# A hybrid attention, recurrence and expert layer: gate map written to PSUM token by token, and the token rows loaded behind the ring in the last stage

## Chip, core and metric

The kernel runs on one core of one Trainium2 chip. The metric is the time of one execution on the device in microseconds, as the median of several runs.

## What is computed

The layer mixes 1024 tokens of width 1024 (attention over a neighbourhood, a recurrence, gates), and then sends each token through PEER: product keys choose 16 of 16384 single-neuron experts for each of 8 heads. The part that matters here is the second:

```python
expert = jnp.take_along_axis(cand_i, pos, axis=-1)          # (token, head, 16)
gate = jax.nn.softmax(best_s, axis=-1)
...
act = jax.nn.gelu(jnp.einsum('td,thkd->thk', hc, u[ec]))    # u: 16384 x 1024
return jnp.einsum('thk,thkd->td', gc * act, v[ec])          # v: 16384 x 1024
...
x = x + gate2[:, None, :] * y
```

## The kernel before

Everything is float32. A product of high precision is made of three matmuls on operands that are split into a high and a low part (`product3`, lines 80 to 82): ScalarE copies the high part, VectorE subtracts it for the low one.

The experts form a 128 x 128 grid, so expert number = 128 x chunk + place. Of the eight tiles of 128 tokens, six are "dense" (768 tokens): for these every one of the 16384 activations is computed, and a gate map, which is zero where an expert was not chosen, picks out what counts. The other two tiles are "gathered": for each of their 128 chosen experts a row of u, and later of v, is fetched by an indirect DMA from GpSimd (lines 1476 and 1840), and VectorE forms the dot products or the weighted sum.

**Stage `activate_and_select`** goes through 128 chunks of u. Chunks 12 to 119 are six bodies of 18 chunks, one body for each dense tile of tokens. For a chunk, TensorE computes 128 x 768 activations in four quarters of 12 matmuls (`quarter`), ScalarE takes the gelu (line 1499) and copies the high part of a later chunk (line 1495), VectorE subtracts (line 1539). In its spare time VectorE sorts out the chosen experts. In chunks 9 to 16 of a body, called hot (HOT to HOT_END), the gate map of the body's 128 tokens is built: 32 groups of four tokens, four groups in each hot chunk, one after each quarter. For a group, VectorE writes one-hot matrices of four tokens (`hot`, lines 1543 and 1547), TensorE multiplies them, one matmul for each token, into one of two PSUM banks (`ps_g`, line 1751), and ScalarE evicts the bank into `gm` in SBUF, which holds for each of 128 places a row of 128 tokens (line 1513). A float32 matmul appears in the trace as two records, so a group is eight. In ScalarE's program, a hot chunk runs: high part of the chunk two ahead, four evictions, gelu. In VectorE's: one-hots of the first group, low part of the chunk two ahead, then the other one-hots, with row products between them.

**Stage `combine`** goes twice (two halves of the dense tokens) through 128 chunks of v in a ring of four. `load` on the sync engine's queue brings activations, gate map and value rows of a chunk (lines 1809, 1810, 1812). ScalarE and VectorE multiply activation and gate (line 1871) and split both factors (lines 1854, 1856, 1873, 1875), VectorE takes one gathered row (line 1880 in the first pass, with the token's row `tok`), and TensorE does 24 matmuls into `ps_y`. In the last chunk of a pass TensorE also transposes the gathered sums with an identity matrix (`ident`, line 1906). The sync engine's queue runs in the order of the program: loads of chunk 0, token rows (line 1815), loads of chunks 1 to 3, identity (line 1818), 2 MB of residual `x1` (line 1821), then the loads of chunk 4 and on, each when its buffer is free.

Of the kernel before, what the change touches and what calls it, by code (L numbers as in the profile page):

```python
# [60 lines left out]
NK = 128  # L61
# [1284 lines left out]
def activate_and_select(nc, io, keep):  # L1346
# [21 lines left out]
    with ExitStack() as ctx:  # L1368
# [110 lines left out]
        @block.scalar  # L1479
        def _(act):  # L1480
            act.sem_inc(act_done, 2)
            for s in range(2):
                act.sem_inc(a_stored[s], 16)
            act.sem_inc(g_copied, 2)
            act.sem_inc(g_stored, 16 * PARTS)
            for c in range(AHEAD):
                act.wait_ge(u_in[c], 16)
                nc.scalar.activation(u_hi[:, c], u_raw[:, c], ACT.Copy).then_inc(u_hi_done, 1)

            def chunk(base, half, j, extra, ahead=True):  # L1490
                s, n = j % 2, (j + AHEAD) % RING
                if ahead:
                    act.wait_ge(u_in[s], half + 16 * (j // 2 + 2))
                    act.wait_ge(a_ready, base + (j + 2))
                    nc.scalar.activation(u_hi[:, n], u_raw[:, s], ACT.Copy).then_inc(u_hi_done, 1)  # L1495
                extra()
                act.wait_ge(a_ready, base + (j + 3))
                act.wait_ge(a_stored[s], half + 16 * (j // 2 + 1))
                nc.scalar.activation(a[:, s].rearrange("p (h t) -> p h t", h=2), ps_a[:, s, :, 0:W], ACT.Gelu_apprx_tanh).then_inc(act_done, 1)  # L1499

            def exponent(steps, j):
                if j == 4:
                    act.wait_ge(step, steps + 3)
                    nc.scalar.activation(best[:], best[:], ACT.Exp).then_inc(exp_done, 1)

            def evicted(tt, j):
                if j == HOT:
                    act.wait_ge(g_stored, 16 * PARTS * tt + 16 * PARTS)
                if HOT <= j < HOT_END:
                    for q in range(QUARTERS):  # L1510
                        g = (j - HOT) * QUARTERS + q
                        act.wait_ge(g_ready, GROUPS * tt + (g + 3))
                        nc.scalar.activation(gm[:, :, g * GT:(g + 1) * GT],  # L1513
                                             ps_g[:, g % 2].rearrange("p (i t) -> p i t", t=GT), ACT.Copy).then_inc(g_copied, 1)

            def body(tt):
                for j in range(BODY):
                    def extra():
                        exponent(STEPS * tt + STEPS, j)
                        evicted(tt, j)  # L1520
                    chunk(BODY * tt + LEAD, (16 * BODY // 2) * tt + 16 * LEAD // 2, j, extra)

            for j in range(LEAD):
                chunk(0, 0, j, lambda: exponent(0, j))
            with act.Fori(0, HALF_BODIES) as tt:
                body(tt)
            act.wait_ge(used, SEL)
            nc.scalar.activation(dots[:], dots[:], ACT.Gelu_apprx_tanh).then_inc(dots_gelu, 1)
            with act.Fori(HALF_BODIES, DENSE) as tt:
                body(tt)  # L1530
            for j in range(REST):
                chunk(NK - REST, 16 * (NK - REST) // 2, j, lambda: exponent(STEPS * (DENSE + 1), j), j + AHEAD < REST)
# [194 lines left out]
        @block.tensor  # L1727
        def _(pe):
            def quarter(c, j, q):
                s, n = j % 2, j % RING  # L1730
                if q == 0:
                    pe.wait_ge(u_lo_done, c + (j + 1))
                    pe.wait_ge(act_done, c + (j + 1))
                for k in range(q * (KD // 4), (q + 1) * (KD // 4)):
                    for h in range(2):
                        cols = slice(h * W, (h + 1) * W)
                        last = product3(nc, ps_a[:, s, h, 0:W], u_hi[:, n, k], u_lo[:, n, k], keep.dense_hi[:, k, cols], keep.dense_lo[:, k, cols],
                                        k == 0, k == KD - 1)
                if q == 3:
                    last.then_inc(a_ready, 1)  # L1740

            def body(tt):
                for j in range(BODY):
                    for q in range(4):
                        quarter(BODY * tt + LEAD, j, q)
                        if HOT <= j < HOT_END:
                            g = (j - HOT) * QUARTERS + q
                            pe.wait_ge(hot_done, GROUPS * tt + (g + 1))
                            pe.wait_ge(g_copied, GROUPS * tt + (g + 1))
                            for i in range(GT):  # L1750
                                last = nc.tensor.matmul(ps_g[:, g % 2].rearrange("p (n t) -> p n t", t=GT)[:, :, i], one2[:, g % 2, i], one1[:, g % 2, i], start=True, stop=True)  # L1751
                            last.then_inc(g_ready, 1)
                        if j == PARTS and q == 1:
                            pe.wait_ge(step, STEPS * tt + (2 * STEPS - 1))
                            for r in range(3):
                                last = nc.tensor.transpose(ps_t[:, r * P:(r + 1) * P], sel[:, r], ident[:])
                            last.then_inc(t_ready, 1)

            pe.wait_ge(consts_in, 32)
            pe.sem_inc(a_ready, 2)  # L1760
            pe.sem_inc(g_ready, 2)
            for j in range(LEAD):
                for q in range(4):
                    quarter(0, j, q)
            with pe.Fori(0, DENSE) as tt:
                body(tt)
            for j in range(REST):
                for q in range(4):
                    quarter(NK - REST, j, q)


def combine(nc, io, keep):
# [5 lines left out]
    with ExitStack() as ctx:  # L1778
# [23 lines left out]
        def _(sp):  # L1802
# [8 lines left out]
                hold(sp, v_lo_done, c + (h * NK + 1), passed)  # L1811
                sp.dma_start(v_raw[:, s], io["v"][c]).then_inc(v_in[s], 16)  # L1812

            load(0, 0, 0)
            sp.dma_start(tok[:], io["tok_scr"][1]).then_inc(tok_in, 16)  # L1815
            for s in range(1, RING):
                load(0, s, s)
            sp.dma_start(ident[:], io["ident"]).then_inc(consts_in, 16)  # L1818
            for h in range(PASSES):
                cols = slice(h * HALF, (h + 1) * HALF)  # L1820
# [38 lines left out]
        def _(dve):  # L1859
            for h in range(PASSES):  # L1860
                if h == 0:
                    nc.vector.memset(y[:], 0.0).then_inc(y_zero, 1)
                else:
                    dve.wait_ge(y_zero, 1)
                    dve.wait_ge(dots_gelu, 1)
                    nc.vector.tensor_tensor(w[:], dots[:], keep.gate[:, 1], ALU.mult).then_inc(w_done, 1)
                    dve.wait_ge(w_done, 1)
                with dve.Fori(0, NK // RING) as i:
                    for s in range(RING):
# [6 lines left out]
                        col = bass.ds(RING * i + s, 1)  # L1876
                        dve.wait_ge(row_in[s], 16 * i + 16 * (h * (NK // RING) + 1))
                        if h == 0:
                            dve.wait_ge(tok_in, 16)
                            nc.vector.scalar_tensor_tensor(out=row[:, s], in0=row[:, s], scalar=1.0, in1=tok[:], op0=ALU.mult, op1=ALU.mult,  # L1880
                                                           accum_out=dots[:, col]).then_inc(used, 1)
                        else:
                            dve.wait_ge(used, RING * i + (SEL + s))
                            nc.vector.scalar_tensor_tensor(out=y[:], in0=row[:, s], scalar=w[:, col], in1=y[:],
                                                           op0=ALU.mult, op1=ALU.add).then_inc(used, 1)
# [7 lines left out]
        def _(pe):  # L1893
            def chunk(s, count, first, last, h):
                pe.wait_ge(v_lo_done, count)
                pe.wait_ge(wa_lo_done, count)
                if last and h >= 1:
                    pe.wait_ge(used, 2 * SEL)
                if last:
                    pe.wait_ge(consts_in, 16)  # L1900
                for k in range(KD):
                    if first and h >= 1:
                        pe.wait_ge(out_done, KD * (h - 1) + k + 1)
                    end = product3(nc, ps_y[:, k, 0:W], v_hi[:, s, k * P:(k + 1) * P], v_lo[:, s, k * P:(k + 1) * P], wa_hi[:, s], wa_lo[:, s], first, last)
                    if last:
                        nc.tensor.transpose(ps_y[:, k, W:HALF], (keep.y, y)[h][:, k * P:(k + 1) * P], ident[:]).then_inc(y_ready, 1)
                if not last:
                    end.then_inc(y_used, 1)
                else:
                    pe.wait_ge(y_ready, KD * (h + 1))  # L1910
                    pe.sem_inc(y_used, 1)

            for h in range(PASSES):
                done = h * NK + RING
                for s in range(RING):
# [144 lines left out]
```

## Time and profile before

| | |
|---|---|
| median of 3 runs | 3989.53 us (3988.51 to 3992.22) |
| the profiled execution | 3992.22 us, its span 3990.4 us |
| mean granted TensorE clock | 0.962 |
| TensorE / VectorE / ScalarE / GpSimd busy | 92% / 66% / 32% / 15% |
| `activate_and_select` | about 1650 to 2890 us of the span |
| `combine` | 2893.8 us to the end |

Matmuls are pipelined, so their busy times overlap: the distance between the starts of two of them says more than the duration of one. A row of the timeline gives start, duration, engine, line, operation and in brackets how long the engine had been idle and what ended that.

### The profile page before, as it was taken

What the parts mean: (1) busy time and instruction counts of PE and PEld (TensorE: products, weight loads), DVE (VectorE), ACT (ScalarE), POOL (GpSimd) and SP (SyncE); (2) the same over time, 40 slices, a digit from 0 to 9 for tenths busy, and PEclk for the clock granted to TensorE, in tenths of its full rate; (3) what the DMA queues carried; (4) which work ended last, traced back from release to release, by engine and by line L of the source; (5) the groups of instructions that cost most, each with busy time, mean ns of one, the idle gap of its engine ahead of it and who ended that gap; (6) DMA issues with size and microseconds to landing.
All of it is one profiled execution on the core that took longest, in us unless ns stands there. A gap on an engine that the chain in (4) does not pass through costs nothing. (4 is left out here: it accounts for less than half of the span.)

```text
span 3990.4 us, 60965 instructions
## 1 busy us (share of the span) xinstructions
PE 3690.4 (92%) x21732; PEld 3387.2 (85%) x21732; DVE 2620.9 (66%) x5324; ACT 1257.5 (32%) x1742; POOL 595.8 (15%) x516
## 2 busy tenths in 40 slices
PE   6899997988499698999999999999989999999999
PEld 3677775656287597999999999999989999999999
DVE  4133444455533488577777787878677777788887
ACT  2134343445311311223222232222233333333332
POOL 0000000000000000132322223232122222222221
PEclk8999999999699799999999999999989999999999
DMA  7311201011322211575968677786799999999997
GB/s 288 120 59 62 67 30 41 32 55 37 113 104 97 84 38 58 181 227 186 301 200 286 224 267 243 243 262 220 230 382 346 347 348 347 348 364 348 347 348 269
DMA packets 373077, 812.80 MB, mean 204 GB/s; under 512 B 30752, under 2 KB 207776, under 8 KB 369440
## 3 DMA queue, kind: packets, MB, share of 16 engines
q1 hardware_dynamic: 299168, 541.86, 38.9%
q0 software_dynamic: 73728, 268.47, 19.6%
q8 instruction: 121, 1.98, 0.2%
q14 instruction: 60, 0.49, 0.0%
HBM read 680.71 MB, written 129.50 MB: 203 GB/s over the span
## 5 line engine op out<-in xcount | busy, mean ns | idle before, releaser
L80 PE MATMUL s_ps_a<-back_dense_hi,s_u_hi 128*128 128x384 f32 x2048 | 706.3, 345 | 43.4 <-DVE s_u_lo L1539 26.8
L80 PE MATMUL c_ps_y<-c_wa_hi,c_v_hi 128*128 128x384 f32 x2048 | 688.6, 336 | 22.5 <-DVE c_wa_lo L1875 22.5
L82 PE MATMUL s_ps_a<-back_dense_hi,s_u_lo 128*128 128x384 f32 x2048 | 688.8, 336 | 0.0
L81 PE MATMUL s_ps_a<-back_dense_lo,s_u_hi 128*128 128x384 f32 x2048 | 688.4, 336 | 0.0
L81 PE MATMUL c_ps_y<-c_wa_lo,c_v_hi 128*128 128x384 f32 x2048 | 687.1, 336 | 0.0
L82 PE MATMUL c_ps_y<-c_wa_hi,c_v_lo 128*128 128x384 f32 x2048 | 686.8, 335 | 0.0
L1854 ACT ACTIVATE c_v_hi<-c_v_raw 128x1024 fp32r<-128x1024 f32 x256 | 271.8, 1062 | 668.2 <-PE c_ps_y L82 618.8
L1476 POOL DMA_INDIRECT s_row<-in_u_rows,back_expert x128 | 159.5, 1246 | 2095.2 <-DVE back_expert L1641 1663.4
L1873 DVE TENSOR_TENSOR c_v_lo<-c_v_raw,c_v_hi 128x1024 fp32r<-128x1024 f32 x256 | 313.7, 1225 | 203.5 <-ACT c_v_hi L1854 203.3
L80 PEld LDWEIGHTS s_ps_a<-back_dense_hi,s_u_hi 128*128 128x128 f32 x2048 | 387.9, 189 | 45.1 <-DVE s_u_lo L1539 27.0
L80 PEld LDWEIGHTS c_ps_y<-c_wa_hi,c_v_hi 128*128 128x128 f32 x2048 | 386.8, 189 | 24.1 <-DVE c_v_lo L1873 23.6
L81 PEld LDWEIGHTS s_ps_a<-back_dense_lo,s_u_hi 128*128 128x128 f32 x2048 | 388.2, 190 | 0.0
L82 PEld LDWEIGHTS s_ps_a<-back_dense_hi,s_u_lo 128*128 128x128 f32 x2048 | 387.2, 189 | 0.0
L82 PEld LDWEIGHTS c_ps_y<-c_wa_hi,c_v_lo 128*128 128x128 f32 x2048 | 386.8, 189 | 0.0
L81 PEld LDWEIGHTS c_ps_y<-c_wa_lo,c_v_hi 128*128 128x128 f32 x2048 | 386.8, 189 | 0.0
L1539 DVE TENSOR_TENSOR s_u_lo<-s_u_raw,s_u_hi 128x1024 fp32r<-128x1024 f32 x128 | 156.7, 1224 | 261.9 <-ACT s_u_hi L1495 246.7
L1499 ACT ACTIVATE s_a<-s_ps_a 128x768 f32<-128x768 f32 x128 | 103.9, 812 | 524.8 <-PE s_ps_a L82 524.8
L1513 ACT ACTIVATE s_gm<-s_ps_g 128x512 f32<-128x512 f32 x192 | 115.0, 599 | 399.1 <-PE s_ps_g L1751 399.1
L1476 POOL DMA_INDIRECT s_row<-in_v,back_expert x128 | 170.4, 1331 | 428.1 <-DVE back_y L1666 413.4
L1547 DVE TENSOR_SCALAR s_one<-s_iota,s_sel_t 128x128 f32<-128x128 f32 x768 | 213.4, 353 | 0.0
L1751 PE MATMUL s_ps_g<-s_one 128*128 128x128 f32 x1536 | 206.6, 277 | 6.4 <-DVE s_one L1547 5.1
L1751 PEld LDWEIGHTS s_ps_g<-s_one 128*128 128x128 f32 x1536 | 195.4, 191 | 20.1 <-DVE s_one L1547 20.1
(319 smaller groups left out, 6643.4 us busy)
## 6 DMA issues: line engine op xcount, KB each, us to landing
c_v_raw<-in_v SPq DMA_DIRECT2D x256, 512.0 KB, 6.4
s_u_raw<-in_u SPq DMA_DIRECT2D x128, 512.0 KB, 4.7
act_scratch<-s_a SPq DMA_DIRECT2D x128, 384.0 KB, 4.0
gm_scratch<-s_gm SPq DMA_DIRECT2D x48, 1024.0 KB, 9.1
c_a<-act_scratch SPq DMA_DIRECT2D x256, 192.0 KB, 3.5
c_g<-gm_scratch SPq DMA_DIRECT2D x256, 192.0 KB, 4.4
a_w<-in_w_ada SPq DMA_DIRECT2D x24, 1024.0 KB, 7.8
q_raw<-in_w_pq SPq DMA_DIRECT2D x17, 512.0 KB, 3.6
```

Of the source, the lines that this page charges most:

```text
L80: nc.tensor.matmul(out, w_hi, x_hi, start=first, stop=False)
L81: nc.tensor.matmul(out, w_hi, x_lo, start=False, stop=False)
L82: return nc.tensor.matmul(out, w_lo, x_hi, start=False, stop=last)
L1476: gp.indirect_dma_start(out=row[:, n % R], out_offset=None, in_=io["u_rows"] if n < SEL else io["v_rows"], in_offset=bass.IndirectOffsetOn ...
L1499: nc.scalar.activation(a[:, s].rearrange("p (h t) -> p h t", h=2), ps_a[:, s, :, 0:W], ACT.Gelu_apprx_tanh).then_inc(act_done, 1)
L1513: nc.scalar.activation(gm[:, :, g * GT:(g + 1) * GT], ps_g[:, g % 2].rearrange("p (i t) -> p i t", t=GT), ACT.Copy).then_inc(g_copied, 1)
L1539: nc.vector.tensor_tensor(u_lo[:, n], u_raw[:, s], u_hi[:, n].bitcast(F32), ALU.subtract).then_inc(u_lo_done, 1)
L1547: last = nc.vector.tensor_scalar(one1[:, g % 2, i], iota[:], sel_t[:, 0, t:t + 1], sel_t[:, 2, t:t + 1], ALU.is_equal, ALU.mult)
L1751: last = nc.tensor.matmul(ps_g[:, g % 2].rearrange("p (n t) -> p n t", t=GT)[:, :, i], one2[:, g % 2, i], one1[:, g % 2, i], start=True, s ...
L1854: nc.scalar.activation(v_hi[:, s], v_raw[:, s], ACT.Copy).then_inc(v_hi_done, 1)
L1873: nc.vector.tensor_tensor(v_lo[:, s], v_raw[:, s], v_hi[:, s].bitcast(F32), ALU.subtract).then_inc(v_lo_done, 1)
```

## The change

Three edits. In `activate_and_select` a gate matmul writes its 128 columns side by side, so a PSUM bank holds four tokens one after another instead of interleaved. The eviction reads the bank in that order and so writes `gm` token by token, in steps of 128 floats. In `combine` the token rows are loaded behind all four chunks of the ring, and VectorE waits for them once, ahead of its loop, instead of at each row product. TensorE waits for the identity matrix ahead of its first chunk instead of in the last chunk of each pass.

```diff
@@ activate_and_select, ScalarE
-                        nc.scalar.activation(gm[:, :, g * GT:(g + 1) * GT],
-                                             ps_g[:, g % 2].rearrange("p (i t) -> p i t", t=GT), ACT.Copy).then_inc(g_copied, 1)
+                        nc.scalar.activation(gm[:, :, g * GT:(g + 1) * GT].rearrange("p i t -> p t i"),
+                                             ps_g[:, g % 2].rearrange("p (t i) -> p t i", t=GT), ACT.Copy).then_inc(g_copied, 1)
@@ activate_and_select, TensorE
                             for i in range(GT):
-                                last = nc.tensor.matmul(ps_g[:, g % 2].rearrange("p (n t) -> p n t", t=GT)[:, :, i], one2[:, g % 2, i], one1[:, g % 2, i], start=True, stop=True)
+                                last = nc.tensor.matmul(ps_g[:, g % 2, i * NK:(i + 1) * NK], one2[:, g % 2, i], one1[:, g % 2, i], start=True, stop=True)
@@ combine, sync engine
-            load(0, 0, 0)
+            for s in range(RING):
+                load(0, s, s)
             sp.dma_start(tok[:], io["tok_scr"][1]).then_inc(tok_in, 16)
-            for s in range(1, RING):
-                load(0, s, s)
             sp.dma_start(ident[:], io["ident"]).then_inc(consts_in, 16)
@@ combine, VectorE
                 if h == 0:
                     nc.vector.memset(y[:], 0.0).then_inc(y_zero, 1)
+                    dve.wait_ge(tok_in, 16)
...
                         if h == 0:
-                            dve.wait_ge(tok_in, 16)
@@ combine, TensorE
-                if last:
-                    pe.wait_ge(consts_in, 16)
...
+            pe.wait_ge(consts_in, 16)
             for h in range(PASSES):
```

## Rows read from the trace of the kernel before

**Rows 1.** The page: busy us (share of the span) and instructions.
```profile
PE 3690.4 (92%) x21732; PEld 3387.2 (85%) x21732; DVE 2620.9 (66%) x5324; ACT 1257.5 (32%) x1742; POOL 595.8 (15%) x516
```

**Rows 2.** The page's groups: busy us, mean ns | idle before, releaser.
```profile
L80 PE MATMUL s_ps_a<-back_dense_hi,s_u_hi 128*128 128x384 f32 x2048 | 706.3, 345 | 43.4 <-DVE s_u_lo L1539 26.8
L80 PE MATMUL c_ps_y<-c_wa_hi,c_v_hi 128*128 128x384 f32 x2048 | 688.6, 336 | 22.5 <-DVE c_wa_lo L1875 22.5
...
L1513 ACT ACTIVATE s_gm<-s_ps_g 128x512 f32<-128x512 f32 x192 | 115.0, 599 | 399.1 <-PE s_ps_g L1751 399.1
```

**Rows 3.** Timeline across the border of two hot chunks, three engines.
```profile
1980.60 1.05 PE L1751 MATMUL s_ps_g<-s_one 128*128 128x128 f32 x8
1981.69 0.60 ACT L1513 ACTIVATE s_gm<-s_ps_g 128x512 f32<-128x512 f32 x1 [2.38 <-PE s_ps_g L1751]
1982.19 0.81 ACT L1499 ACTIVATE s_a<-s_ps_a 128x768 f32<-128x768 f32 x1
1982.88 1.06 ACT L1495 ACTIVATE s_u_hi<-s_u_raw 128x1024 fp32r<-128x1024 f32 x1
...
1983.58 1.05 PE L1751 MATMUL s_ps_g<-s_one 128*128 128x128 f32 x8
1983.97 1.22 DVE L1539 TENSOR_TENSOR s_u_lo<-s_u_raw,s_u_hi 128x1024 fp32r<-128x1024 f32 x1 [2.31 <-ACT s_u_hi L1495]
...
1985.11 0.68 DVE L1543 TENSOR_TENSOR s_one<-s_iota,s_sel_t 128x512 f32<-128x512 f32 x1
...
1986.88 1.16 PE L1751 MATMUL s_ps_g<-s_one 128*128 128x128 f32 x8 [0.15 <-DVE s_one L1547]
```

**Rows 4.** Timeline, TensorE: first and last of 42 groups after a long step.
```profile
1799.64 1.16 PE L1751 MATMUL s_ps_g<-s_one 128*128 128x128 f32 x8 [0.15 <-DVE s_one L1547]
...
2807.79 1.16 PE L1751 MATMUL s_ps_g<-s_one 128*128 128x128 f32 x8
```

**Rows 5.** Timeline, start of combine, all engines.
```profile
2904.50 0.66 PE L80 MATMUL c_ps_y<-c_wa_hi,c_v_hi 128*128 128x384 f32 x1 [14.68 <-DVE c_wa_lo L1875]
...
2905.76 0.94 POOL L1840 DMA_INDIRECT c_row<-in_u_rows,back_expert  x1 [6.84 <-DVE c_row L1880]
...
2912.00 0.41 PE L80 MATMUL c_ps_y<-c_wa_hi,c_v_hi 128*128 128x384 f32 x1 [0.45 <-DVE c_wa_lo L1875]
...
2912.91 0.55 DVE L1871 TENSOR_TENSOR c_g<-c_g,c_a 128x384 f32<-128x384 f32 x1
...
2914.75 1.07 ACT L1854 ACTIVATE c_v_hi<-c_v_raw 128x1024 fp32r<-128x1024 f32 x1 [0.72 <-DMA c_v_raw<-in_v]
...
2924.39 0.34 PE L82 MATMUL c_ps_y<-c_wa_hi,c_v_lo 128*128 128x384 f32 x1
...
2925.47 1.06 ACT L1854 ACTIVATE c_v_hi<-c_v_raw 128x1024 fp32r<-128x1024 f32 x1 [8.22 <-DMA c_v_raw<-in_v]
...
2926.56 1.23 DVE L1873 TENSOR_TENSOR c_v_lo<-c_v_raw,c_v_hi 128x1024 fp32r<-128x1024 f32 x1 [2.45 <-ACT c_v_hi L1854]
...
2927.70 0.55 DVE L1875 TENSOR_TENSOR c_wa_lo<-c_g,c_wa_hi 128x384 fp32r<-128x384 f32 x1
...
2928.40 0.66 PE L80 MATMUL c_ps_y<-c_wa_hi,c_v_hi 128*128 128x384 f32 x1 [3.67 <-DVE c_wa_lo L1875]
```

**Rows 6.** Busy time by stretch of the span; last come granted clock, DMA share, GB/s.
```profile
2904.00:2908.00 4.00, 3.50 (x11) 3.53 (x12) 2.05 (x4) 0.00 (x0) 0.94 (x1) 0.50 1.02 398
...
2928.00:2932.00 4.00, 3.60 (x11) 3.63 (x12) 4.00 (x7) 2.64 (x3) 1.01 (x1) 0.50 1.04 409
```

**Rows 7.** Timeline, TensorE: five records of gate matmuls, five of routing scores.
```profile
1784.52 0.72 PE L1751 MATMUL s_ps_g<-s_one 128*128 128x128 f32 x5
...
1380.15 0.72 PE L1333 MATMUL q_score<-q_keys,q_q 128*128 x5
```

**Rows 8.** Groups by shape, ScalarE: contiguous copies of 1024 and 512 columns.
```profile
L1495 ACT ACTIVATE s_u_hi<-s_u_raw 128x1024 fp32r<-128x1024 f32 x126 | 132.8, 1054 | 3.4 <-DMA s_u_raw<-in_u 3.4
...
L1288 ACT ACTIVATE q_q<-q_acc 128x512 f32<-128x512 f32 x32 | 19.1, 598 | 177.1 <-PE q_acc L82 177.1
```

## Prediction

> **What bounds the kernel now.** I read the page first. TensorE is busy for 92% of the span [rows 1], and the groups put its idle time before the matmuls of the two stages that the change touches at 43.4 us and 22.5 us [rows 2]. So in both stages TensorE sets the time, and anything is worth what it adds to or takes from TensorE's gaps. The groups also give the gate map's eviction, 192 instructions of 599 ns, with ScalarE idle for 399.1 us before them: by busy time alone it looks free.
>
> Then the timeline, around one eviction that ends a chunk. Where nothing interferes, one group of four gate matmuls follows the last at 2.98 us (1980.60 to 1983.58), the two 12-matmul pieces between them included. But the next group starts 3.30 us later (1986.88). The reader is to see in [rows 3] that the rows behind this touch each other: the group of 1980.60 ends and ScalarE evicts it (1981.69), then takes the gelu (1982.19), then splits the next u chunk (1982.88); VectorE, which is in order and waits at that point for the split, subtracts (1983.97), builds the one-hots (1985.11), and TensorE's second group of the chunk waits for those (1986.88). None of these steps has slack. The same long step, 3.29 to 3.30 us, comes 42 times, seven in each of the six bodies: once in every hot chunk but the first of a body, the first at 1799.64 and the last at 2807.79 [rows 4]. So the eviction that closes a hot chunk is on TensorE's path, and each nanosecond on it is paid 42 times; the other 150 of the 192 have slack (a bank is wanted again two groups, 6 us, later).
>
> Last, the start of combine. TensorE starts at 2904.50, has a gap of 0.45 us before chunk 1 (2912.00) and a second of 3.8 us before chunk 4 (2924.39 to 2928.40), because the value rows of chunk 4 landed only at 2925.47 [rows 5]. The DMA engines are full meanwhile, 398 to 409 GB/s [rows 6].
>
> **Part 1, the matmul's output.** Its elements stood 16 bytes apart in PSUM, and stand side by side after the change. What is that worth? The trace has both forms with the same tile: five records of the strided one take 0.72 us, and five of the routing scores', whose output is contiguous, take 0.72 us as well [rows 7]. Eight of the strided ones take 1.05 us [rows 3], so three more add 0.33: 0.11 us each, and the contiguous ones come as fast. I take 0 for the gain.
>
> The Trainium skill says otherwise: "Advanced Engine Details and Errata", section Memory Cachelines, has it that any non-contiguous pattern in PSUM slows matmuls significantly. These rows disagree with it for this stride, and I follow the rows; what it would give is a rival below.
>
> **Part 1, the eviction.** It still reads 512 contiguous floats of PSUM. Before, it wrote runs of four floats, a run every 512 bytes; after, each float goes 512 bytes from the one before it. Nothing in this trace writes so. The bounds: from below, no change; ScalarE's 512-column copies that write contiguously take 598 ns, against 599 for runs of four, so jumping every fourth element costs nothing [rows 2, 8]. From above: 1024 columns take 1054 ns and 512 take 598, so an element costs 0.89 ns and the rest is 0.14 us. If a jump were as slow as it can be while runs of four still hide it, it would take the time of four elements, and the eviction 0.14 + 512 x 3.56 ns = 1.97 us. Between 1 and 4 element times per element I take 2, the geometric middle: the eviction lasts as long as a 1024-column copy, 1.054 us, which is 0.456 us more. Paid where? ScalarE's gelu and split start 0.456 us later, VectorE's subtraction and one-hots too, and TensorE's second group of the next chunk: **42 x 0.456 = 19.2 us**. The other 150 are covered, since ScalarE waits 2.1 us ahead of an eviction in the mean (399.1 / 192, [rows 2]); without that cover they would cost as much each. No DMA waits for the eviction before the next body.
>
> The Trainium skill speaks against this edit, on the same page and section: SBUF's lines have 16 bytes, at least two hits on one are needed to absorb the memory's latency, and a different line at each access is penalised. It gives no price. No row here shows it; if two hits are just enough, one hit per line would mean two element times, and the sum would be the same 19.2 us.
>
> **Part 2, combine's loads and waits.** The token rows go from behind the first chunk's loads to behind those of the fourth, and VectorE waits for them ahead of everything, where only its row product had. Behind that wait stand the gating, the splits and so TensorE. The queue moves the same bytes by then: chunk 3's value rows landed at 2914.7 with the token rows ahead of them [rows 5]. After, the token rows are last and land there, less the time of one gathered row set: the fifth was issued at 2905.76, and now waits for VectorE's first product. It is 128 x 4 KB = 0.52 MB, at some 400 GB/s 1.3 us. So the wait ends at about 2913.3. Then come gating 0.56, subtraction (1.14 until the next starts) and 0.70 from there to TensorE's first matmul [rows 5]: TensorE starts at 2915.7 instead of 2904.50, 11.2 us later.
>
> Not all of this stays. Meanwhile the loads of chunks 1 to 3 have landed, so TensorE has no gap at chunk 1. Chunk 0 takes 7.05 us at the low granted clock (0.50, 1.2 GHz, as it was after 14.7 us of idle) [rows 5, 6]; chunks 1 to 3 took 12.56 us at the high one. It reaches chunk 4 at 2915.7 + 7.0 + 12.6 = 2935.3. Chunk 4's value rows landed 10.7 us behind chunk 3's (2914.75 to 2925.47), and were ready for TensorE 2.9 us later; that gives about 2927, so the 3.8 us gap goes too, and with it the second stretch at 0.50, which made chunk 4 take 7.0 instead of 4.2. Chunk 4 ends at 2939.5, before at 2928.4 + 7.0 = 2935.4. **Part 2 costs 4.1 us.** If the fifth row set did not hold the queue up, 5.4. VectorE needs 0.55 + 1.23 + 0.55 and a product of the size of the subtraction, 3.6 us, for each chunk against TensorE's 4.2, so it stays ahead.
>
> The wait for the identity matrix now stands ahead of chunk 0. It is 64 KB right behind the token rows, and covered by the 2.4 us that VectorE takes after them; if not, each us would be paid once. The 127 waits for the token rows that go from the loop lie on VectorE, which is ahead of TensorE: nothing.
>
> **Sum.** 19.2 + 4.1 = 23.3 us. The profiled execution took 3992.22 us (span 3990.4 and 1.8 around it), so it would be 4015.5; the median of the runs is 2.7 lower, 3989.53, and gives 4012.8.
>
> **The rivals.** (a) A float every 512 bytes costs ScalarE nothing. For it: runs of four cost nothing. Then only part 2 is left: 3989.5 + 4.1 = 3993.6, which cannot be told from no change. (b) It costs three element times or more, up to four: 42 x 1.37 = 57.5, and 4051. For it: nothing bounds it tighter. (c) The other side: contiguous outputs do make the gate matmuls faster, beyond what [rows 7] show for two different stages. Each group shorter by y shortens a chunk with a long step by 3y (its path holds one group, the other two stand beside it) and saves y in each of the other 24, in all 150 y. It decides against my sum from y = 23.3 / 150 = 0.155 us, 19 ns of each of the eight records' 111. If a record halved, y = 0.44 and the kernel took 66 us less, 3947 with the eviction's cost. Against it: the equal 0.72 us. This is where the Trainium skill's rule on non-contiguous PSUM patterns (same page and section) would lead. (d) The gap before chunk 4 stays, because its loads, queued behind 2 MB of residual and issued 11 us later, land later: 3.8 us and the second slow stretch of 2.8 come back, 4019.4. For it: the queue is full; against it: 8 us of margin.
>
> **How the numbers follow.** Forecast 0.50, with values near two element times; (a) 0.20; (b) 0.15; (c) 0.05; (d) 0.10. About 0.2%, 8 us, can be told from no change. Faster is (c), 0.05. Within 0.2% is (a) without (d), and a little of the forecast's lower edge: 0.20. Slower is the rest, 0.75. The range starts at 3991, which takes in (a), and ends at 4024, which takes in (d) and an eviction of up to 1.32 us; it leaves out (c) and (b). The forecast's own range is 4006 to 4020.
>
> **What would show it.** Right: the eviction's mean near 1.05 us; the gate matmuls' records still 0.11 us apart; the long step 3.75 instead of 3.30, with VectorE's wait for ScalarE's split grown by the same; TensorE's first matmul in combine some 25 us after its last of the stage before, and one gap there instead of three. Wrong: an eviction still at 0.60 us (a), gate matmuls closer together (c), or a long step that does not grow by what the eviction grows, which would mean slack that I have not seen.

## The result, and the profile after

The changed kernel takes 4012.54 us in the median of four runs (4011.00 to 4019.09) against 3990.61 us of the kernel before in the same comparison: a ratio of 1.0059, 95% interval 1.0043 to 1.0076. It is slower by 17 to 30 us. The execution that was profiled is one of the slower ones, 4018.81 us with a span of 4017.0, so its span stands 26.6 us above that of before, where the medians stand 22 apart; the last section says where the rest of that lies.

These are the page's groups of the changed kernel that answer to [rows 2] (busy us, mean ns | idle before, releaser).

```profile
L80 PE MATMUL c_ps_y<-c_wa_hi,c_v_hi 128*128 128x384 f32 x2048 | 687.2, 336 | 30.0 <-DVE c_wa_lo L1875 30.0
...
L1513 ACT ACTIVATE s_gm<-s_ps_g 128x512 f32<-128x512 f32 x192 | 213.0, 1109 | 324.7 <-PE s_ps_g L1751 324.7
...
L1751 PE MATMUL s_ps_g<-s_one 128*128 128x128 f32 x1536 | 206.5, 277 | 24.0 <-DVE s_one L1547 24.0
```

The row of the gate matmuls in the kernel before, for comparison:

```profile
L1751 PE MATMUL s_ps_g<-s_one 128*128 128x128 f32 x1536 | 206.6, 277 | 6.4 <-DVE s_one L1547 5.1
```

The eviction went from 599 to 1109 ns. The gate matmuls' busy time, 206.6 us before, is 206.5 us: the contiguous output gave nothing. But TensorE now waits 24.0 us for one-hots, which the kernel before kept to 5.1 us.

The timeline across the border of two hot chunks, after, answers to [rows 3]:

```profile
1982.47 1.05 PE L1751 MATMUL s_ps_g<-s_one 128*128 128x128 f32 x8
1983.56 1.08 ACT L1513 ACTIVATE s_gm<-s_ps_g 128x512 f32<-128x512 f32 x1 [1.85 <-PE s_ps_g L1751]
1984.44 0.85 ACT L1499 ACTIVATE s_a<-s_ps_a 128x768 f32<-128x768 f32 x1
1985.18 1.05 ACT L1495 ACTIVATE s_u_hi<-s_u_raw 128x1024 fp32r<-128x1024 f32 x1
...
1985.45 1.05 PE L1751 MATMUL s_ps_g<-s_one 128*128 128x128 f32 x8
...
1986.26 1.23 DVE L1539 TENSOR_TENSOR s_u_lo<-s_u_raw,s_u_hi 128x1024 fp32r<-128x1024 f32 x1 [2.79 <-ACT s_u_hi L1495]
...
1987.40 0.69 DVE L1543 TENSOR_TENSOR s_one<-s_iota,s_sel_t 128x512 f32<-128x512 f32 x1
...
1989.17 1.16 PE L1751 MATMUL s_ps_g<-s_one 128*128 128x128 f32 x8 [0.58 <-DVE s_one L1547]
```

The rows touch each other as they did before. The undisturbed step is still 2.98 us (1982.47 to 1985.45), the long one is 3.72 (1985.45 to 1989.17) where it was 3.30. The gelu starts 0.88 us behind the eviction instead of 0.50, and the high part 0.74 behind the gelu instead of 0.69: those two make the 0.42 to within a hundredth. TensorE's idle time on the last row grew from 0.15 to 0.58 us. From the first gate group of a body to its last it is 98.3 to 98.4 us in all six bodies, before 95.4 to 95.6: 2.9 us for each body's seven long steps, 17.4 us in all.

The start of combine, after, answers to [rows 5]. Times in this stage are counted from its first load, here in the kernel before and then, with the rows behind it, in the changed one:

```profile
2893.82 0.34 SPq L1809 DMA_DIRECT2D c_a<-act_scratch  x1
```

```profile
2916.22 0.34 SPq L1809 DMA_DIRECT2D c_a<-act_scratch  x1
...
2936.26 0.56 DVE L1871 TENSOR_TENSOR c_g<-c_g,c_a 128x384 f32<-128x384 f32 x1 [19.05 <-DMA c_tok<-tok_scratch]
...
2936.73 1.22 DVE L1873 TENSOR_TENSOR c_v_lo<-c_v_raw,c_v_hi 128x1024 fp32r<-128x1024 f32 x1
2937.87 0.55 DVE L1875 TENSOR_TENSOR c_wa_lo<-c_g,c_wa_hi 128x384 fp32r<-128x384 f32 x1
...
2938.56 0.66 PE L80 MATMUL c_ps_y<-c_wa_hi,c_v_hi 128*128 128x384 f32 x1 [26.34 <-DVE c_wa_lo L1875]
```

VectorE stands for 19 us until the token rows land, and TensorE for 26.3 us instead of 14.7. It starts 22.3 us behind the stage's first load, before 10.7 (2893.82 to 2904.50). Then it does not stop again in this pass. The identity matrix, for which TensorE now waits ahead of chunk 0 as well, landed at 2936.2 (issued at 2923.6, 12.6 us to landing), 2.4 us before TensorE could start, so this wait cost nothing. The windows (answer to [rows 6]; the third number from the end is the granted clock) show a single stretch at the low level:

```profile
2936.00:2940.00 4.00, 1.44 (x5) 1.47 (x6) 3.75 (x7) 1.47 (x2) 0.17 (x1) 0.50 1.00 379
2940.00:2944.00 4.00, 4.00 (x15) 4.00 (x14) 4.00 (x7) 2.18 (x4) 1.79 (x2) 0.54 0.97 341
2944.00:2948.00 4.00, 4.00 (x25) 4.00 (x24) 4.00 (x8) 2.24 (x3) 1.08 (x2) 1.00 1.02 364
```

From the stage's first load to the end of the span it is 1100.8 us (4017.0 - 2916.22), before 1096.6 (3990.4 - 2893.82): 4.2 us more, although the start came 11.7 us later.

### The profile page after: what moved, and what is told of

Same layout as the page of the kernel before. It is cut to its first block and busy times, and to the rows that moved or that the text cites. A ratio compares the mean times of both kernels' runs of the same rounds, so it can differ in the third digit from the quotient of the medians.

```text
span 4017.0 us, 60836 instructions
## 1 busy us (share of the span) xinstructions
PE 3693.0 (92%) x21732; PEld 3390.0 (84%) x21732; DVE 2620.9 (65%) x5324; ACT 1351.8 (34%) x1742; POOL 597.3 (15%) x516
## 5 line engine op out<-in xcount | busy, mean ns | idle before, releaser
L80 PE MATMUL s_ps_a<-back_dense_hi,s_u_hi 128*128 128x384 f32 x2048 | 709.2, 346 | 42.6 <-DVE s_u_lo L1539 26.6
L80 PEld LDWEIGHTS c_ps_y<-c_wa_hi,c_v_hi 128*128 128x128 f32 x2048 | 385.8, 188 | 31.1 <-issue 26.6
L1513 ACT ACTIVATE s_gm<-s_ps_g 128x512 f32<-128x512 f32 x192 | 213.0, 1109 | 324.7 <-PE s_ps_g L1751 324.7
L1751 PE MATMUL s_ps_g<-s_one 128*128 128x128 f32 x1536 | 206.5, 277 | 24.0 <-DVE s_one L1547 24.0
```

The lines of the kernel that those rows point to most:

```text
L80: nc.tensor.matmul(out, w_hi, x_hi, start=first, stop=False)
L1513: nc.scalar.activation(gm[:, :, g * GT:(g + 1) * GT].rearrange("p i t -> p t i"), ps_g[:, g % 2].rearrange("p (t i) -> p t i", t=GT), ACT. ...
L1751: last = nc.tensor.matmul(ps_g[:, g % 2, i * NK:(i + 1) * NK], one2[:, g % 2, i], one1[:, g % 2, i], start=True, stop=True)
```

## The experiments

Twelve kernels ran, each timed in five rounds against the kernel before. All diffs are against the kernel before unless said otherwise.

### The two parts apart

**gate_only** has the first two hunks of the change (matmul output and eviction), **combine_only** the other three.

> Only the gate map's part of the change (contiguous matmul outputs, eviction that writes a float every 512 bytes). My theory: the eviction of 1.11 us closes each hot chunk and is paid 42 times by 0.41 us, the amount by which the long step between gate groups grew (3.30 to 3.71 us): +17.5 us, some 4008. The 192 evictions' means stay 1.11 us. Rival, in which the extra time comes from what the eviction does to the loop seams or the clock: more than +20 us here, with long steps that explain less than it. Rival, in which combine's part is the larger one: under +10 us.

> Only combine's part of the change (token rows behind four chunks' loads, both waits at the front). My theory: TensorE starts its first matmul of combine some 11.5 us later after the stage's first load than before, but has no gap at chunks 1 and 4 and one stretch at the low granted clock instead of two: +4 us, some 3994.6. Rival, in which the late start is paid in full: +11 us. Rival, in which it is hidden by the DMA queue's time: 0.

gate_only: 4010.29 us, ratio 1.0040 (1.0026 to 1.0054), so +10 to +22 us. Its evictions and long steps are those of the whole change; a body is 98.3 us long. combine_only: 3996.09 us, ratio 1.0006 (0.9997 to 1.0015), so -1 to +6 us. This interval holds zero and 4 us, and leaves out 11. In its trace TensorE starts 22.2 us behind the first load (2896.59 to 2918.84), has no second gap, and the stage is 1100.2 us long. The stage's length in three kernels with the new combine (the whole change, combine_only, and late_after below) is 1100.8, 1100.2 and 1099.8 us. In the seven with the old one (before, gate_only, scatter_last, scatter_others, late_before, read_strided, scatter_interleaved) it is 1096.6, 1097.2, 1097.3, 1096.7, 1095.9, 1099.1 and 1097.6, a mean of 1097.2. So the traces put this part at 3 us, one execution to the next differing by 1 or 2.

### Which evictions cost

The new layout, matmul and eviction, for a quarter or for three quarters of the groups. **scatter_last** takes it for the group that closes a hot chunk, **scatter_others** for the other three (`q < QUARTERS - 1`).

```diff
@@ ScalarE (TensorE's output is chosen by the same condition)
-                        nc.scalar.activation(gm[:, :, g * GT:(g + 1) * GT],
-                                             ps_g[:, g % 2].rearrange("p (i t) -> p i t", t=GT), ACT.Copy).then_inc(g_copied, 1)
+                        fresh = q == QUARTERS - 1
+                        nc.scalar.activation(gm[:, :, g * GT:(g + 1) * GT].rearrange("p i t -> p t i") if fresh else gm[:, :, g * GT:(g + 1) * GT],
+                                             ps_g[:, g % 2].rearrange("p (t i) -> p t i", t=GT) if fresh else ps_g[:, g % 2].rearrange("p (i t) -> p i t", t=GT),
+                                             ACT.Copy).then_inc(g_copied, 1)
```

> The new layout for the last gate group of each hot chunk alone (48 of 192 evictions), the old one for the other three. My theory, only the closing eviction is on TensorE's path: nearly all of the gate part's cost, +17 us, some 4008, long steps of 3.7 us. Rival, every longer eviction costs alike through ScalarE's load: a quarter, +4 us.

> The new layout for the first three gate groups of each hot chunk (144 of 192 evictions), the old one for the closing group. My theory: they have 2 us of ScalarE's idle time ahead of each, so 0 within 1 us, long steps still 3.30 us. Rival, every longer eviction costs alike: three quarters, +13 us.

scatter_last: 4008.70 us, ratio 1.0045 (1.0031 to 1.0059). scatter_others: 3992.56 us, ratio 1.0001 (0.9992 to 1.0010). The 48 closing evictions cost what all 192 cost; the other 144 cost nothing that can be measured. The tile's row and the list of TensorE's waits, first for scatter_last (min/median/max of the evictions in ns; then us in total, times, longest us):

```profile
L1514 ACT ACTIVATE s_gm<-s_ps_g x192: 597/600/1139, 1787.4 to 2830.2; 128x512 f32<-128x512 f32 x192
...
PE s_ps_g L1754 <- DVE s_one L1549: 24.0, 42, 0.6
```

and for scatter_others:

```profile
L1514 ACT ACTIVATE s_gm<-s_ps_g x192: 597/1112/1157, 1786.6 to 2816.4; 128x512 f32<-128x512 f32 x192
...
PE s_ps_g L1754 <- DVE s_one L1549: 6.0, 39, 0.2
```

In the first, the median eviction is as short as before and TensorE still waits 24.0 us; in the second the median is 1112 ns and it waits 6.0 us. ScalarE's load does not decide, the place does.

### What makes the eviction slow

**read_strided** has the contiguous matmul output, and an eviction that walks in the old order: it writes runs of four and so reads PSUM at every 128th float. **scatter_interleaved** has the old matmul output and the scattered write, and reads PSUM at every fourth float.

```diff
@@ read_strided, ScalarE (TensorE has the changed kernel's matmul)
-                                             ps_g[:, g % 2].rearrange("p (i t) -> p i t", t=GT), ACT.Copy).then_inc(g_copied, 1)
+                                             ps_g[:, g % 2].rearrange("p (t i) -> p i t", t=GT), ACT.Copy).then_inc(g_copied, 1)
@@ scatter_interleaved
-                        nc.scalar.activation(gm[:, :, g * GT:(g + 1) * GT],
-                                             ps_g[:, g % 2].rearrange("p (i t) -> p i t", t=GT), ACT.Copy).then_inc(g_copied, 1)
+                        nc.scalar.activation(gm[:, :, g * GT:(g + 1) * GT].rearrange("p i t -> p t i"),
+                                             ps_g[:, g % 2].rearrange("p (i t) -> p t i", t=GT), ACT.Copy).then_inc(g_copied, 1)
```

> Contiguous matmul outputs as after the change, but the eviction writes runs of four floats as before, and so reads PSUM at every 128th float. Theory, the scattered write is what is slow: the eviction takes 0.60 us and the kernel the time of before, 3990. Rival, the order of the loops (innermost runs of four on either side) or a strided access on either side costs: the eviction stays at 1.1 us or takes yet another time, and the kernel is at +17 us.

> Interleaved matmul outputs as before, and the eviction writes a float every 512 bytes as after, reading PSUM at every fourth float. Theory, the write alone sets the eviction's time and the layout of the matmul's output costs TensorE nothing: eviction 1.11 us, kernel +17.5 us, some 4008, the same as the gate part alone. Rival, contiguous matmul outputs gave something back in the gate part alone: this one is slower than it by more than 3 us. Rival, two strided sides add up: eviction longer than 1.11 us.

The group of the eviction in read_strided:

```profile
L1513 ACT ACTIVATE s_gm<-s_ps_g 128x512 f32<-128x512 f32 x192 | 114.9, 598 | 399.1 <-PE s_ps_g L1751 399.1
```

and in scatter_interleaved, with its gate matmuls:

```profile
L1513 ACT ACTIVATE s_gm<-s_ps_g 128x512 f32<-128x512 f32 x192 | 213.0, 1109 | 324.5 <-PE s_ps_g L1751 324.5
...
L1751 PE MATMUL s_ps_g<-s_one 128*128 128x128 f32 x1536 | 206.5, 277 | 24.1 <-DVE s_one L1547 24.1
```

read_strided: 3992.01 us, ratio 1.0000 (0.9991 to 1.0009). scatter_interleaved: 4010.62 us, ratio 1.0045 (1.0031 to 1.0058). Between these layouts the write alone decides: reads of PSUM at every 128th float (with runs of four written) and at every fourth (with single floats written) cost nothing, and the matmuls' busy time is 206.5 us with either layout. Only two writes were tried, runs of four floats and single floats, both with a jump of 512 bytes. Whether runs of two, or single floats a shorter way apart, would be as slow is not shown. The contiguous matmul output is worth nothing in either pair, (before, read_strided) and (scatter_interleaved, gate_only).

### The eviction off the path

If the chain of the prediction is right, the eviction can be taken out of it. **late_before** evicts the closing group of a hot chunk behind the gelu and the next high part instead of ahead of them; **late_after** is the changed kernel with the same edit.

```diff
-                if HOT <= j < HOT_END:
-                    for q in range(QUARTERS):
+                if HOT <= j <= HOT_END:
+                    for q in range(-1, QUARTERS - 1):
                         g = (j - HOT) * QUARTERS + q
+                        if g < 0 or g >= GROUPS:
+                            continue
```

> The kernel before, with ScalarE's eviction of a hot chunk's last gate group moved behind the gelu and the next high part. My theory, a path eviction, gelu, high part, low part, one-hots closes the long steps: gelu and high part then start about 1.1 us earlier, the long step (3.30) and the one after it (3.10) fall to 2.98 us, and 42 times 0.44 us go: -18 us, some 3972. Rival, the long step is the one-hots' own work on VectorE (four groups, two row products and a low part in a chunk): nothing moves.

> The changed kernel with the same move of the eviction. My theory: the slower eviction is now covered, so this stands to the moved one of before only by combine's part, +4 us: some 3976, which is 36 us less than the changed kernel. Rival, a slower eviction costs on TensorE wherever it stands (by its memory accesses or by holding the PSUM bank): some 17 us above the moved one of before.

late_before: 3972.46 us, ratio 0.9949 (0.9936 to 0.9963). late_after: 3976.58 us, 0.9962 (0.9949 to 0.9976). In both, each body is 92.4 us from first to last gate group, the 31 steps of 2.98 us and nothing else. This takes 18.4 us off the six bodies of the kernel before, more than the 42 x 0.32 of the long steps: each long step had a second one behind it, 3.08 to 3.11 us, and that falls to 2.98 too. Here is the border of two hot chunks in late_after:

```profile
1976.91 1.05 PE L1753 MATMUL s_ps_g<-s_one 128*128 128x128 f32 x8
1977.11 0.81 ACT L1499 ACTIVATE s_a<-s_ps_a 128x768 f32<-128x768 f32 x1 [0.95 <-PE s_ps_a L82]
1977.82 1.05 ACT L1495 ACTIVATE s_u_hi<-s_u_raw 128x1024 fp32r<-128x1024 f32 x1
...
1978.77 1.11 ACT L1515 ACTIVATE s_gm<-s_ps_g 128x512 f32<-128x512 f32 x1
1978.90 1.23 DVE L1541 TENSOR_TENSOR s_u_lo<-s_u_raw,s_u_hi 128x1024 fp32r<-128x1024 f32 x1 [0.99 <-ACT s_u_hi L1495]
...
1979.89 1.05 PE L1753 MATMUL s_ps_g<-s_one 128*128 128x128 f32 x8
...
1982.88 1.05 PE L1753 MATMUL s_ps_g<-s_one 128*128 128x128 f32 x8
```

The eviction is as slow as in the changed kernel, 1.11 us, but the subtraction no longer waits for it, and the second group comes after 2.99 us. What is left between the two kernels is 4.1 us between the medians and 3.9 us between the lengths of the stage `combine` in their traces (1099.8 and 1095.9), combine's part. So the slow write as such costs TensorE nothing.

### Combine's part taken apart

**tok_wait_front** only moves the wait for the token rows ahead of VectorE's loop; **tok_load_late** only moves their load behind the fourth chunk's. **residual_mid** is about the gap ahead of chunk 4: the 2 MB of the residual are loaded in the middle of each pass.

```diff
@@ residual_mid: sync engine, `combine`
+                with sp.Fori(1, NK // RING // 2) as i:
+                    for s in range(RING):
+                        load(h, sp.snap(RING * i + s), s)
                 sp.dma_start(x1[:], io["x1_scr"][:, :, cols].rearrange("k p t -> p k t")).then_inc(x1_in, 16)
-                with sp.Fori(1, NK // RING) as i:
+                with sp.Fori(NK // RING // 2, NK // RING) as i:
```

> The kernel before, with VectorE's wait for the token rows ahead of its loop, but the rows still loaded behind the first chunk. Their landing is at 9.8 us of the stage there, against the 8.9 us at which VectorE could start its first subtraction. Theory: TensorE's first matmul moves from 10.7 us after the stage's first load to about 12.2, and the gaps at chunks 1 and 4 stay, since the loads behind are where they were: +1 to +2 us. Rival: the wait itself is what costs combine's 4 us, +4.

> The kernel before, with the token rows loaded behind all four chunks but the wait still in the loop. Theory: TensorE takes chunk 0 early, as before (10.7 us after the first load), then waits for chunk 1 until the token rows' landing at about 19.8 us and VectorE's work behind it (near 24 us), a gap of some 6 us; then the loads of chunk 4 are there sooner than TensorE needs them. In all between -2 and +3 us. Rival: landing late costs what it costs with the front wait, +4.

> The kernel before, with the 2 MB load of the residual moved from ahead of chunk 4's loads to the middle of each pass. Theory, the second gap of TensorE in combine (3.8 us ahead of chunk 4, and 2.8 us of low granted clock behind it) comes from that load: both go, 5 to 6.5 us less, some 3985; and in the middle the ring's lead covers its 5 us. Rival, the ring's loads are late because the DMA engines are full with gathered rows anyway: a gap of 3 us or more stays ahead of chunk 4.

tok_wait_front: 3992.01 us, ratio 0.9999 (0.9990 to 1.0008). TensorE starts 12.9 us behind the first load (2895.29 to 2908.18). The gap ahead of chunk 4 stays, but the one ahead of chunk 1, which was expected to stay too, is gone; its next stop is this one:

```profile
2931.18 0.66 PE L80 MATMUL c_ps_y<-c_wa_hi,c_v_hi 128*128 128x384 f32 x1 [4.32 <-DVE c_wa_lo L1876]
```

tok_load_late: 3992.84 us, ratio 1.0004 (0.9995 to 1.0013). TensorE starts 11.4 us behind the first load, then stands ahead of chunk 1 for the token rows; this is TensorE's second start in the timeline of tok_load_late, and it has no gap ahead of chunk 4:

```profile
2913.77 0.66 PE L80 MATMUL c_ps_y<-c_wa_hi,c_v_hi 128*128 128x384 f32 x1 [5.57 <-DVE c_wa_lo L1874]
```

By the runs neither half can be told from no change. The front wait alone costs at most 3 us, so it is not what costs 4; the late load alone costs at most 5. The stage's lengths in their traces are 1097.5 and 1096.9 us, inside those of the old combine. That it takes both halves to cost 3 to 4 us is shown by the traces alone, not by the medians. In each of the twelve traces without the edit of residual_mid, the time from TensorE's first matmul of chunk 5 to the end of the span is 1055.1 to 1055.2 us, so whatever the stage gains or loses is settled by then. These are the starts of chunks, in us behind the stage's first load, counted off in the timeline (a chunk has 24 matmuls for `ps_y`):

| kernel | chunk 0 | chunk 1 | chunk 5 |
|---|---|---|---|
| before | 10.7 | 18.2 | 41.5 |
| tok_wait_front | 12.9 | 18.9 | 42.4 |
| tok_load_late | 11.4 | 23.7 | 41.8 |
| combine_only | 22.3 | 28.4 | 45.0 |
| the changed kernel | 22.3 | 29.0 | 45.6 |

With the old combine, chunk 5 starts at 40.8 to 44.0. With the late load alone, TensorE has chunk 0 behind it when it comes to wait for the token rows, and does not run dry at chunk 4. With the front wait alone, the token rows are there at 10.3 us. Only with both does chunk 0 itself wait for rows that land at 20 us. The wait for the identity matrix was not tried alone.

residual_mid: 3986.49 us, ratio 0.9986 (0.9977 to 0.9995), and a stage of 1092.0 us. Its list of waits (us in total, times, longest us) has 20.4 us for TensorE in 3 waits where the kernel before has 22.5 us in 4, and none ahead of chunk 4 (the third lies between the passes, 3.7 us as in the kernel before):

```profile
PE c_ps_y L80 <- DVE c_wa_lo L1878: 20.4, 3, 15.2
```

```profile
2903.94 0.66 PE L80 MATMUL c_ps_y<-c_wa_hi,c_v_hi 128*128 128x384 f32 x1 [15.23 <-DVE c_wa_lo L1878]
2911.75 0.41 PE L80 MATMUL c_ps_y<-c_wa_hi,c_v_hi 128*128 128x384 f32 x1 [1.52 <-DVE c_wa_lo L1878]
```

### Both gains together

**late_residual** has the edits of late_before and residual_mid.

> The kernel before with both: the closing eviction behind the next high part, and the residual's load in the middle of the pass. Theory, the two gains lie in different stages and add: -18 and -5 to -6.5, some 3966. Rival, they do not add: 3970 or more.

It takes 3964.92 us, ratio 0.9933 (0.9919 to 0.9946): 27 us less than the kernel before and 48 less than the changed one. The gains add, within the noise: the interval is 22 to 32 us less than before.

## Why the prediction was right, by its own steps

**Which eviction is paid.** The prediction said 42 times, once in every hot chunk but a body's first, and nothing for the other 150. Shown: scatter_last takes 1.0045 times the kernel before and scatter_others 1.0001 times; TensorE's waits for one-hots are 24.0 us in 42 places in the first and 6.0 us in the second.

**The size of the eviction.** It had no row for it and took 2 element times, the geometric middle between bounds of 1 and 4, for 1.054 us. Measured 1.109: (1109 - 142) / 512 = 1.89 ns an element, 2.1 element times. The bounds were worked out from rows; that the truth lay so near their middle is luck. The Trainium skill ("Advanced Engine Details and Errata", section Memory Cachelines) says that SBUF has lines of 16 bytes and that at least two hits on one are needed to absorb the latency. The traces agree as far as they go: runs of four floats cost nothing in read_strided, single floats twice the time in scatter_interleaved. Runs of two, where the rule has its border, were not tried.

**The term of 19.2 us.** It was a little too large: 17.4 us in the lengths of the six bodies. Two misses of opposite sign are in it. The eviction grew by 0.51 us, where 0.456 was assumed; paid in full, that would have been 21.4 us. But ScalarE starts its next instruction before the end of the last, 0.10 us before it in [rows 3] and 0.20 us in the changed kernel (1983.56 + 1.08 against 1984.44). So the chain lengthened by the distance between starts, 0.38 us, and by 0.04 to 0.05 behind the gelu. What sits on a path is the distance to the next start, not the duration. Why the overlap doubled is open.

**What it missed on this path.** It named the 42 long steps only. The step behind each long one was also above 2.98 us, 3.08 to 3.11, in both kernels. That changed nothing in the sum, but the eviction's place was worth more than the 42 x 0.32 us that the prediction's rows show, as late_before found.

**The matmul's output, 0.** Right: 206.6 us of busy time before, 206.5 after, and scatter_interleaved equals gate_only within the noise. Rival (c) is out. The Trainium skill's rule that any non-contiguous pattern in PSUM slows matmuls significantly (same page and section) is not borne out by these float32 matmuls at a stride of four floats.

**Combine, 4.1 us.** VectorE's wait for the token rows was to end 19.5 us behind the stage's first load (2913.3 - 2893.8) and ended at 20.0 (2936.26 - 2916.22). TensorE's start was to move by 11.2 us and moved by 11.7. The two later gaps and the second stretch at the low clock went, as forecast. The prediction counted to the end of chunk 4 and had 4.1 us there; in the profiled pair chunk 5 starts 4.15 us later (41.45 and 45.60 us behind the first load). The stage grew by 4.2 us in this pair, by 3 in the mean of the traces, and by -1 to +6 in combine_only's runs. One size was off: chunk 0 at the low clock was taken at 7.05 us and took 6.6, 6.1 and 5.6 us in the changed kernel, combine_only and late_after, since the granted clock came back to 1.00 after a shorter time there. Rival (d) is out: in the changed kernel, combine_only and late_after no gap stays ahead of chunk 4. That the gap of the kernel before came from the 2 MB of the residual in the queue ahead of chunk 4's loads is shown by residual_mid.

**The sum.** 23.3 us forecast, 21.9 between the medians, 23.5 by the ratio of 1.0059. Of this the traces account for 17.4 and 3 to 4. The median, 4012.54, lies 0.3 us from the forecast of 4012.8; so near a hit is luck, for the sum is 1.4 us larger than the difference of the medians, and the median of before from which it was counted, 3989.53, is 1.1 us lower than the one of the comparison.

## What to carry to other kernels

An engine that is busy a third of the time can still set the pace: look at the order of its instructions where a waiting, in-order engine behind it feeds TensorE, and move out of that order what nobody there needs. When a float32 tile has to be transposed between PSUM and SBUF, put the jumps on the matmul's output or on ScalarE's read of PSUM and keep the write to SBUF in runs of 16 bytes; here that took 598 ns where single floats took 1109. And a late start is not paid in full if it lets a buffer fill that ran dry later: of 11.7 us, 4.2 were left.

## What had not been expected

**The seam between bodies.** TensorE stands for 3.1 to 4.0 us at each turn of the loop of bodies, with nothing that the profile shows as a reason. What follows differs from turn to turn in one and the same execution. In the kernel before, after the turn at 2266:

```profile
2266.33 0.41 PE L80 MATMUL s_ps_a<-back_dense_hi,s_u_hi 128*128 128x384 f32 x1 [3.06 <-issue]
```

```profile
2266.00:2270.00 4.00, 3.67 (x21) 3.70 (x22) 3.85 (x6) 0.00 (x0) 1.14 (x1) 1.00 1.06 358
```

and in the changed kernel after a stop of the same length at 2084:

```profile
2084.42 0.66 PE L80 MATMUL s_ps_a<-back_dense_hi,s_u_hi 128*128 128x384 f32 x1 [3.13 <-issue]
```

```profile
2084.00:2088.00 4.00, 3.58 (x11) 3.61 (x12) 4.00 (x6) 0.00 (x0) 1.14 (x1) 0.50 1.08 362
```

The granted clock was 1.00 (the 2.4 GHz level) after the first stop (3.06 us) and 0.50 (1.2 GHz) after the second (3.13 us). The first is the exception in its execution: in the kernel before, the 4 us behind the other four stops (from 1892, 2079, 2451 and 2639) have a mean granted clock of 0.63 to 0.73. From the last gate group of a body to the first of the next it is 88.7 to 93.9 us over all kernels here. The five seams together are 456.8 us in the profiled execution of before and 462.6 in that of the changed kernel; in gate_only, which has the same code in this stage, they are 456.8, and in the other eleven traces 452.8 to 457.6. So this is the execution's luck and not the change's doing. What decides it was not tried. With this the 26.6 us between the two profiled spans are complete: 17.4 in the bodies, 5.8 in the seams, 4.2 in combine, and 0.8 less ahead of the first gate group.

**Two element times.** A ScalarE copy of 512 columns that writes one float every 512 bytes takes 1109 ns, whether it reads PSUM contiguously or at every fourth float; in runs of four floats it takes 598, even when it reads PSUM at every 128th.
